# Gate and up of a transformer feed-forward layer: feature-major chunks, or Strassen products and token-major stretches

## The reference

```python
h = rms_norm(x, ffn_norm_g[layer])
x = x + (jax.nn.silu(h @ w_ffn_gate[layer]) * (h @ w_ffn_up[layer])) @ w_ffn_down[layer]
return rms_norm(x, final_norm_g)
```

## Time and profile before

| | us |
|---|---|
| median of 3 runs (388.69 to 389.08) | 388.72 |
| span of the profiled execution, first to last instruction | 387.1 |
| median less span: what lies around it | 1.6 |
| PE busy | 379.2 |
| DVE busy | 249.4 |
| ACT busy | 199.1 |

### The profile page before, as it was taken

One profiled execution on the slowest core, in us unless ns is written; L12 is line 12 of the kernel. 1 busy time (PEld: TensorE's weight loads), 2 busy tenths in 40 slices (PEclk: granted clock), 3 DMA queues, 4 the chain that ended last, 5 costly groups with the idle time before them and its releaser, 6 DMA issues.

```text
span 387.1 us, 5211 instructions
## 1 busy us (share of the span) xinstructions
PE 379.2 (98%) x2027; PEld 324.8 (84%) x2027; DVE 249.4 (64%) x335; ACT 199.1 (51%) x249; POOL 35.7 (9%) x37
## 2 busy tenths in 40 slices
PE   7999999999999999999999999999999999999993
PEld 6998888788888888888888888888888888888883
DVE  4999968974474872699757672744738366482326
ACT  4766796763492631743456463461725437163015
POOL 2797020000000040000100000000000000000001
PEclk9999999999999999999999999999999999999998
DMA  8996366947148196167536756639174472930002
GB/s 277 272 314 230 108 198 213 327 138 256 66 118 317 31 392 230 40 203 217 193 108 235 233 183 219 205 122 315 60 275 152 173 255 74 321 108 1 0 2 108
DMA packets 47369, 70.55 MB, mean 182 GB/s; under 512 B 2252, under 2 KB 30968, under 8 KB 47352
## 3 DMA queue, kind: packets, MB, share of 16 engines
q1 hardware_dynamic: 47136, 70.03, 53.6%
q10 hardware_dynamic: 216, 0.28, 0.2%
HBM read 69.26 MB, written 1.05 MB: 182 GB/s over the span
## 4 chain that ended last, share of the span: by engine, by line
PE 97%; issue 1%; DVE 1%; POOL 0%; ACT 0%; POOLq 0%; ACTq 0%; DVEq 0%
PE pa L1228 21%; PE pp L1237 13%; PE pp L1238 13%; PE pp L1239 13%; PE pa L1230 11%; PE pp L1228 4%; PE pp L1217 3%; PE pp L1230 2%; PE pa L1238 2%; PE pa L1239 2%; PE pa L1237 2%; PE pp L1258 1%; PE pa L1521 1%; PE pa L1523 1%; PE pa L1522 1%; PE pa L1339 1%
## 5 line engine op out<-in xcount | busy, mean ns | idle before, releaser
L784 DVE TENSOR_TENSOR w_lo<-w_raw,w_hi 128x2048 fp32r<-128x2048 f32 x38 | 86.3, 2292 | 19.6 <-ACT w_hi L467 19.6
L1228 PE MATMUL pa<-hT,w_hi 128*128 128x512 f32 x352 | 87.9, 392 | 0.0
L467 ACT ACTIVATE w_hi<-w_raw 128x2048 fp32r<-128x2048 f32 x38 | 71.9, 1916 | 22.2 <-DMA w_raw<-in_w_in 9.3
L1228 PEld LDWEIGHTS pa<-hT,w_hi 128*128 128x128 f32 x352 | 63.9, 189 | 11.9
L1168 DVE TENSOR_TENSOR w_lo<-w_raw,w_hi 128x2048 fp32r<-128x2048 f32 x24 | 53.6, 2287 | 8.9 <-ACT w_hi L737 8.9
L1230 PEld LDWEIGHTS pa<-hT,w_lo 128*128 128x128 f32 x352 | 48.0, 190 | 3.4
L1237 PE MATMUL pp<-w_hi,hT 128*128 128x512 f32 x128 | 50.5, 395 | 0.0
L1239 PE MATMUL pp<-w_lo,hT 128*128 128x512 f32 x128 | 49.9, 390 | 0.0
L1238 PE MATMUL pp<-w_hi,hT 128*128 128x512 f32 x128 | 49.8, 389 | 0.0
L1230 PE MATMUL pa<-hT,w_lo 128*128 128x256 f32 x352 | 49.1, 282 | 0.0
L737 ACT ACTIVATE w_hi<-w_raw 128x2048 fp32r<-128x2048 f32 x24 | 44.1, 1899 | 0.0
(11 more groups left out here) (254 smaller groups left out, 466.9 us busy)
## 6 DMA issues: line engine op xcount, KB each, us to landing
w_raw<-in_w_in SPq DMA_DIRECT2D x21, 1024.0 KB, 5.3
w_raw<-in_w_ffn_gate SPq DMA_DIRECT2D x11, 1024.0 KB, 5.4
w_raw<-in_w_ffn_up SPq DMA_DIRECT2D x11, 1024.0 KB, 6.2
w_raw<-in_w_ffn_down SPq DMA_DIRECT2D x11, 1024.0 KB, 6.4
w_raw<-in_w_o SPq DMA_DIRECT2D x4, 1024.0 KB, 5.9
w_raw<-in_w_out_attn SPq DMA_DIRECT2D x2, 1024.0 KB, 5.0
w_raw<-in_w_out_mlstm SPq DMA_DIRECT2D x2, 1024.0 KB, 5.0
x_sb<-in_x SPq DMA_DIRECT2D x2, 512.0 KB, 3.9
```

Of the source, the lines that this page charges most:

```text
L467: nc.scalar.activation(w_hi[:, slot_of(c), :], w_raw[:, c % RAW, :], ACT.Copy).then_inc(hi_ready, 1)
L784: nc.vector.tensor_tensor(w_lo[:, slot_of(c), :], w_raw[:, c % RAW, :], w_hi[:, slot_of(c), :].bitcast(F32), ALU.subtract).then_inc(lo_rea ...
L1228: mm(banks[:, f, :], w_hi[:, s, w[k]], hT[:, k], start=(k == 0), stop=False)
```

## The change

The 11 stretches of 256 features are dealt out anew. Five are computed token-major like the first one before ("plain" 0 to 4, each followed by 4 transposes). The other six form three "sets" of 512 features. For a set, tokens (2 tiles x 2 halves of the 1024 inputs) times [gate | up] (2 halves x 2) is a 2 x 2 block product, which is done with seven block products instead of eight (B11, T1, T2, B22, T3, B21, T4; 12 matmuls of 512 columns each). Four of them use differences of weight blocks, T1 = B12 - B11, T2 = B22 - T1, T3 = B22 - B12, T4 = B21 - T2, each formed by DVE over 128 x 2048 and then split by ACT and DVE like a chunk. The four block sums of the tokens are formed once and split once (`hS`). ACT copies partial products out of PSUM (`keep`), DVE adds (`add_part`), and the gated product of a set is transposed by 8 transposes (`set_turn`). The down product keeps its 24 matmuls a stretch (dA, dB of the set before, dN of a plain stretch; dB of set 0 doesn't exist). A fourth raw buffer is laid over `v_att` and `o_sb`. The loops are replaced by unrolled code. FORMS is the order in which the ring is filled and used; ACT and DVE split the form six places ahead when they handle the one at hand (`following`). `plain(n)` waits for `plain_lo_set` from n = 3 on; `down` is the 24 matmuls as before. AT gives a form's place in the ring, LANDED its raw buffer.

```diff
-FG = F // 256
-FIRST = 0
+SETS = 3
+PLAIN = 2 + SETS
+FORMS = ("B11", "T1", "dA", "T2", "B22", "dB", "T3", "B21", "dN", "T4", "NG", "NU")
+SUMS = ("T1", "T2", "T3", "T4")
 QUARTERS = tuple(slice(D // 4 * n, D // 4 * (n + 1)) for n in range(4))
...
+def forms_of(p):
+    if p == SETS:
+        return ("dA", "dB", "dN")
+    return tuple(n for n in FORMS if p or n != "dB")
...
+def set_column(p):
+    return 512 + 768 * p
+def plain_column(n):
+    return 256 * n if n < 2 else 1024 + 768 * (n - 2)
...
+            def load_form(p, name, done, value):
+                buf = LANDED[p, name][0]
+                src = set_source(p, name)
+                sp.wait_ge(done, value)
+                sp.dma_start(as_source(raw_of(buf), src), src).then_inc(chunk_loaded[buf], 16)
+            for p in range(SETS):
+                if p == 0:
+                    load_form(p, "B11", lo_ready, C_FFN + 2)
+                    load_form(p, "B12", lo_ready, C_FFN + 3)
+                    load_form(p, "B22", normed, 4)
+                    load_form(p, "dA", lo_ready, C_FFN + 4)
+                else:
+                    load_form(p, "B11", w_summed, 4 * p)
+                    load_form(p, "B12", lo_ready, AT[p - 1, "dN"] + 1)
+                    load_form(p, "B22", lo_ready, AT[p - 1, "NG"] + 1)
+                    load_form(p, "dA", lo_ready, AT[p - 1, "NU"] + 1)
+                    load_form(p, "dB", lo_ready, AT[p, "B11"] + 1)
+                load_form(p, "B21", lo_ready, AT[p, "dA"] + 1)
+                load_form(p, "dN", w_summed, 4 * p + 3)
+                load_form(p, "NG", lo_ready, AT[p, "dB" if p else "B11"] + 1)
+                load_form(p, "NU", lo_ready, AT[p, "T3"] + 1)
+            load_form(SETS, "dA", w_summed, 4 * SETS)
+            load_form(SETS, "dB", lo_ready, AT[SETS - 1, "dN"] + 1)
+            load_form(SETS, "dN", lo_ready, AT[SETS - 1, "NG"] + 1)
...
+            def form_hi(p, name):
+                c = AT[p, name]
+                if name in SUMS:
+                    act.wait_ge(w_summed, 4 * p + SUMS.index(name) + 1)
+                else:
+                    act.wait_ge(chunk_loaded[LANDED[p, name][0]], LANDED[p, name][1])
+                act.wait_ge(chunk_used, c - RING + 1)
+                nc.scalar.activation(w_hi[:, slot_of(c), :], form_raw(p, name), ACT.Copy).then_inc(hi_ready, 1)
+            def plain_gate(n, used):
+                act.wait_ge(chunk_used, used)
+                nc.scalar.activation(hid_n[:, :].rearrange("p (t n) -> p t n", t=T), plain_banks(n)[:, :, 0:256],
+                                     ACT.Silu).then_inc(plain_silu, 1)
+            def plain_hi(n):
+                act.wait_ge(plain_turned, n + 1)
+                f = plain_yT(n)
+                nc.scalar.activation(yT_hi[:, f:f + 2, :], pa[:, 3, :].rearrange("p (f n) -> p f n", f=2), ACT.Copy
+                                     ).then_inc(plain_hi_set, 1)
+            def keep(part, bank, used):
+                act.wait_ge(chunk_used, used)
+                nc.scalar.activation(part, pa[:, bank, :], ACT.Copy).then_inc(part_kept, 1)
+            nc.scalar.activation(sum4, pa[:, 0, :], ACT.Copy)
+            act.wait_ge(hT_lo_set, 16)
+            nc.scalar.activation(sum2, pp[:, 1, :], ACT.Copy).then_inc(h_copied, 1)
+            form_hi(0, "B11")
+            act.wait_ge(h_summed, 4)
+            nc.scalar.activation(hS[:, 0, :, :].rearrange("p f n -> p (f n)"), region_a[:, :], ACT.Copy
+                                 ).then_inc(hS_hi_set, 1)
+            plain_gate(0, C_FFN + 2)
+            form_hi(0, "T1")
+            plain_hi(0)
+            form_hi(0, "dA")
+            form_hi(0, "T2")
+            plain_gate(1, C_FFN + 4)
+            form_hi(0, "B22")
+            form_hi(0, "T3")
+            following = {c - RING: form for form, c in AT.items()}
+            for p in range(SETS):
+                for name in forms_of(p):
+                    c = AT[p, name]
+                    if name == "B11":
+                        if p == 0:
+                            act.wait_ge(hS_lo_set, 1)
+                        keep(gate0, 0, c + 1)
+                    elif name == "T1":
+                        keep(up1, 1, c + 1)
+                    elif name == "T2":
+                        keep(up0, 0, c + 1)
+                    elif name == "T3":
+                        plain_hi(p + 1)
...
+                    elif name == "NU":
+                        plain_gate(p + 2, c + 1)
+                        if c - 1 in following:
+                            form_hi(*following[c - 1])
+                    if name != "NG" and c in following:
+                        form_hi(*following[c])
+                    if name == "B21":
+                        act.wait_ge(part_added, 3 * p + 3)
+                        nc.scalar.activation(gate0, gate0, ACT.Silu).then_inc(set_silu, 1)
+            plain_hi(PLAIN - 1)
...
+            dve.wait_ge(h_copied, 1)
+            nc.vector.tensor_tensor(sum1, pp[:, 0, :], sum2, ALU.add).then_inc(h_summed, 1)
+            nc.vector.tensor_tensor(sum3, sum4, pp[:, 0, :], ALU.subtract).then_inc(h_summed, 1)
+            dve.wait_ge(h_summed, 1)
+            nc.vector.tensor_tensor(sum2, sum1, sum4, ALU.subtract).then_inc(h_summed, 1)
+            dve.wait_ge(h_summed, 3)
+            nc.vector.tensor_tensor(sum4, pa[:, 1, :], sum2, ALU.subtract).then_inc(h_summed, 1)
             split_lo(C_FFN + 3)
...
+            def form_lo(p, name):
+                c = AT[p, name]
+                dve.wait_ge(hi_ready, c + 1)
+                nc.vector.tensor_tensor(w_lo[:, slot_of(c), :], form_raw(p, name),
+                                        w_hi[:, slot_of(c), :].bitcast(F32), ALU.subtract).then_inc(lo_ready, 1)
+            def form_sum(p, name):
...
+                nc.vector.tensor_tensor(form_raw(p, name), raw_of(LANDED[p, first][0]), with_, ALU.subtract
+                                        ).then_inc(w_summed, 1)
...
+            def add_part(part, bank, used, kept):
+                dve.wait_ge(chunk_used, used)
+                dve.wait_ge(part_kept, kept)
+                nc.vector.tensor_tensor(part, pa[:, bank, :], part, ALU.add).then_inc(part_added, 1)
+            form_sum(0, "T1")
+            form_lo(0, "B11")
+            plain_product(0)
+            form_lo(0, "T1")
+            plain_lo(0)
+            dve.wait_ge(hS_hi_set, 1)
+            nc.vector.tensor_tensor(hS[:, 1, :, :].rearrange("p f n -> p (f n)"), region_a[:, :],
+                                    hS[:, 0, :, :].rearrange("p f n -> p (f n)").bitcast(F32), ALU.subtract
+                                    ).then_inc(hS_lo_set, 1)
+            form_sum(0, "T2")
+            form_lo(0, "dA")
+            plain_product(1)
+            form_lo(0, "T2")
+            form_lo(0, "B22")
+            form_sum(0, "T3")
+            form_lo(0, "T3")
+            following = {c - RING: form for form, c in AT.items()}
+            def next_lo(c):
+                if c not in following:
+                    return
+                p, name = following[c]
+                form_lo(p, name)
+                if name == "T1":
+                    form_sum(p, "T2")
+                elif name == "B22":
+                    form_sum(p, "T3")
+                elif name == "B21":
+                    form_sum(p, "T4")
+            for p in range(SETS):
+                for name in forms_of(p):
+                    c = AT[p, name]
+                    if name == "B22":
+                        add_part(up0, 1, c + 1, 3 * p + 3)
+                        if p == 0:
+                            form_sum(1, "T1")
+                    elif name == "dB" and p + 1 < SETS:
+                        form_sum(p + 1, "T1")
+                    elif name == "T3":
+                        plain_lo(p + 1)
+                        add_part(up1, 0, c + 1, 3 * p + 2)
+                    elif name == "B21":
+                        add_part(gate0, 1, c + 1, 3 * p + 1)
+                    elif name == "dN":
+                        dve.wait_ge(set_silu, 2 * p + 1)
+                        dve.wait_ge(part_added, 3 * p + 1)
+                        nc.vector.tensor_tensor(gate0, gate0, up0, ALU.mult).then_inc(set_prod, 1)
+                    elif name == "T4":
+                        dve.wait_ge(set_silu, 2 * p + 2)
+                        dve.wait_ge(part_added, 3 * p + 2)
+                        nc.vector.tensor_tensor(gate1, gate1, up1, ALU.mult).then_inc(set_prod, 1)
...
+                    elif name == "NU":
+                        plain_product(p + 2)
+                        next_lo(c - 1)
+                    if name != "NG":
+                        next_lo(c)
+            plain_lo(PLAIN - 1)
...
+            def product(p, name, bank, a_hi, a_lo, start):
+                c = AT[p, name]
+                s = slot_of(c)
+                pe.wait_ge(lo_ready, c + 1)
+                o = pa[:, bank, :]
```

(85 more changed lines are left out.)

270 lines of the change are left out of this document (126 added, 144 removed).

## The result

| | us |
|---|---|
| before, median of the runs beside it | 388.89 |
| after, median of 4 runs (397.62 to 401.20) | 399.21 |
| ratio | 1.0269, interval 1.0231 to 1.0307 |
| profiled execution: its time, its span | 397.96, 396.2 |

The change makes the kernel slower, as forecast, but by 10.3 us and not by 6.1: the median lies 1.2 us above the top of the range. The same kernel on another chip, with five rounds, gave 397.92 (396.31 to 399.75), ratio 1.0235, interval 1.0214 to 1.0257, just inside it. What follows goes by profiled executions; I measure the feed-forward part from the start of its first matmul to 0.12 us, one step of a 256-column matmul, after the start of its last. Before takes 183.94 us in it (197.15 to 381.09) and after 192.29 (197.47 to 389.76).

What follows compares the result with a forecast made beforehand. The prediction took the kernel to be bound by the number and shape of PE's matmuls. PE's work -6.3, set 0 slip +10.5 and set 1 slip +1.9 gave +6.1 on 388.72: 394.8 us, range 392.4 to 398.0.

Steps and rivals of the forecast that it cites:

- The mechanism: DVE's queue up to plain_lo(1) makes PE late at set 0's dN by 10.5 us, set 1 by 1.9, set 2 none.
- the faster rival: DVE's weight sums run at double rate in SBUF, slip 5.0 in place of 10.5, total 387.5 us; chance 0.08.
- the falling clock as a rival: Set 0's pauses of 3.4 and 3.5 us halve PE's clock; 2.5 us lost after dN's pause, total 397.3; chance 0.12.
- a granted clock under 1.00 near 255: Listed sign that the forecast is wrong: PE's clock reduced around the start of set 0's dN; no size given.
- Its other half: Slow matmuls after set 0's first long pause are harmless, since DVE decides when dN starts.
- the 14 forecast: Sign of being right: PE's list of waits holds about 14 us, 2 before, the longest before set 0's dN.
- the load of B12: Set 1's sum T1 in DVE's queue waits 1.2 us for this load; the same again in set 1 for the next.
- hS at no cost: Matmuls with hS stationary were charged nothing extra in PE's work; bound 0 to +0.2 us.
- 6.3 forecast for PE's work: PE's feed-forward matmuls and transposes together: -10.9 for matmuls, +1.7 and +2.9 for transposes, so -6.3 us.
- Late loads: 1.5 us more on each of the two B12 loads goes straight to the end, total 398 us; chance 0.08.
- A partly hidden backlog: DVE reaches block sums earlier or full-width items overlap, net near zero, total 389 to 392 us; chance 0.07.

Runs made afterwards that it cites:

- the reordered kernel: Changed kernel with T1 sums of sets 1 and 2 formed later, and ACT's and DVE's set 0 queues ordered as PE wants them: 383.91 us, ratio 0.9878.
- the kernel with the later T1: Changed kernel with the next set's sum T1 moved behind plain_lo(p+1) and the add of up1 in DVE's queue: 390.39 us, ratio 1.0042.
- the kernel with one split too many: Changed kernel with DVE doing T2's split of set 0 twice: 401.42 us, ratio 1.0312.

## Why the prediction was right in direction and too low

**The mechanism was right.** PE leaves its place as the bound for some 60 us, DVE's queue sets when `down(0, dN)` starts, its sums run at single rate (2.28 forecast, 2.28 measured, so the faster rival falls), set 1 has one small pause and set 2 none. The forecast put `plain_lo(1)`'s end at 253.0 and dN at 253.1; they are at 253.8, of which 0.32 is a later start of the whole part. One queued instruction more cost 2.46 where 2.3 was expected. The Trainium skill ("VectorE: DVE Perf Modes", "The perf-mode tier table") holds a float32 two-tensor operation within SBUF at the single rate, and the sums' 2.28 us agree.

**The step that failed is the clock, left out of the sum.** The forecast's own working had pauses of 3.4 and 3.5 us and a row in which the clock falls 2.4 us after PE's last matmul, and still gave the falling clock as a rival with 0.12. By its own numbers the condition was met in the likeliest case. It had named a granted clock under 1.00 near 255 as a sign of being wrong, and 254 to 256 shows 0.77. The runs show the fall in both profiled executions of the changed kernel; its price, forecast as 2.5, is 1.65 to 1.7 there, and probably more in the longer ones, whose mean clock is lower. Its other half was right: the slow matmuls after the pause before T3 cost 0.3 us at most, for they fill the pauses forecast before B21 (1.6, measured none) and dN (3.5, measured 2.56). That is also why PE's list of waits holds 10.9 us and not the 14 forecast. The Trainium skill ("TensorE: Matmul & The Clock Gate", "Why this matters for your kernels") warns that the clock falls back when matmuls pause. The trace agrees, and the fall came with pauses of 2.9 and 2.6 us, shorter than those that the page warns of.

**Smaller terms.** The median lies 4.4 us above the forecast (399.21 against 394.8). The feed-forward part grew by 8.35 where 6.1 was forecast. Up to dN of set 0 that is 0.4 more (56.35 us from the first matmul against 55.95), since the load of B12 held DVE for 1.64 against 1.2. Behind it it is 1.85: clock 1.7, the hS matmuls of set 2 0.3, less 0.3 because set 1's load wait was 0.88 and not 1.2; 0.15 stay open. Around the part lie 0.32 and 0.43. The 0.32 is a later start of the part; the same kernel started it at 197.47 in one execution and at 197.07 in the other. The 0.43 lies behind the issue of the last store (3.44 us to the end of the span in place of 3.01); no run asks why. What lies around the span was 1.76 and not 1.6. That gives the profiled 397.96. The median of the first measurement stands 1.25 above its profiled execution, the repeated one 0.2; that part goes with the clock, as said above, and is not shown to come from it.

**hS at no cost was wrong.** The bound was +0.2 by the pitch of a `down`; the 144 matmuls cost 0.95, 0.0066 us more each, where the tile lies now. In the changed kernel the two thirds ahead of the waits of sets 0 and 1 are hidden in them. In the reordered kernel it is most of the gap between 5.0 measured and 6.3 forecast for PE's work; the remaining 0.3 was not tried. The first matmuls after a switch are 0.31 apart in place of 0.23, and those with hT late in set 0 0.231 in place of 0.2267; either could be it.

**Late loads** as a rival did not come (0.4 more on one, 0.3 less on the other). **A partly hidden backlog** didn't come by itself either, but it was the true offer of this change: with the queues reordered, 5 us are gained, and the order as written spent them and 9 more, nearly all in set 0.

## What to carry to other kernels

When an added backlog decides, list the queue up to the instruction that the bottleneck waits for, and ask of every item ahead of it whether it is wanted later or waits for a load: moving one such item in two sets was worth 7.5 us here, reordering set 0 on top of it 14 in all, with not one instruction less. Taking an item out is worth only the distance to the next limit (a load, the other engine's half of a split); read that limit's time before you count the gain. If your own working holds pauses on PE as long as one after which a row shows the clock fallen, the clock belongs in the sum: here slow matmuls ahead of the last pause cost 0.3 us at most, those behind it 1.7.

## What the runs showed of the hardware

The clock of TensorE fell from 2.4 to 1.2 GHz inside a pause of 2.9 us, with the window 240 to 242 already at 0.85 after a last matmul that started at 239.02, and matmuls were slow until 248. In the kernel with the later T1 the same pause was 2.90 us and the clock stood at 1.00 to its end (240 to 242); the matmuls were slow from 242.1 to 245.1, right behind it. The second time in after they were slow from 255.08 to 258.07, 1.3 us after PE had started again: the fall came later than the pause. A pause of 1.76 us (before T2) and one of 1.19 (set 1) passed with no slow matmul behind them; in the kernel with one split too many a pause of 2.03 us in set 1 was followed by matmuls 0.43 apart from 308.7 to 311.7, and its `down` took 7.15 us against 5.58 behind the pause of 1.19. So pauses of one length were not followed by slow stretches of one length, and the shortest pause with one behind it was 2.03 us.

The same matmul, same shape, type and moving operand, starts every 0.2333 us when its stationary tile lies high in SBUF (behind `v_ml`), and every 0.2267 when it lies low (between `w_raw` and `w_hi`); at the high place it makes no difference whether hi and lo tiles alternate. What it is about the address is open: one place of each kind was tried, and the moving tiles lay 24 KB higher in the second.
